# Decoder trunk layer in split fp32: the weight-half buffers made four deep and the block product regrouped

## The reference

```
h = rmsnorm(x)
parts = split(h @ w_in)                 # 46 tiles of 128 features for four mixers, and 64 of gate logits
o_a, o_b, o_c, o_d = hgrn2(...), diff_attention(...), nsa(...), chunk_gmlp(...)   # 512 wide each
merged = sum_b sigmoid(gate_b) * (o_b @ w_branch[b])
x = x + merged @ w_out
x = x + cross_attention(rmsnorm(x), rmsnorm(mem))     # 4 heads, 256 memory tokens
gate, up = split(rmsnorm(x) @ w_ffn_in) # 5632 each
x = x + (silu(gate) * up) @ w_ffn_out
out = rmsnorm(x)
```

## Time and profile before

| | |
|---|---|
| runs | 2203.86 us median of 3 (2201.33 to 2205.67) |
| profiled execution, span | 2204.4 us (its own time outside the span isn't recorded) |
| PE, PEld busy | 2090.2 us (95%), 1782.6 us (81%) |
| DVE, ACT, POOL busy | 1382.8 us (63%), 936.6 us (42%), 1063.7 us (48%) |
| memory traffic | 378.20 MB, mean 172 GB/s |
| granted TensorE clock | full, but for short stretches in the first 520 us and the end |

### The profile page before, as it was taken

One profiled execution on the slowest core, in us unless ns is written; L12 is line 12 of the kernel. 1 busy time (PEld: TensorE's weight loads), 2 busy tenths in 40 slices (PEclk: granted clock), 3 DMA queues, 4 the chain that ended last, 5 costly groups with the idle time before them and its releaser, 6 DMA issues.

```text
span 2204.4 us, 31459 instructions
## 1 busy us (share of the span) xinstructions
PE 2090.2 (95%) x11734; PEld 1782.6 (81%) x11734; DVE 1382.8 (63%) x1528; ACT 936.6 (42%) x1126; POOL 1063.7 (48%) x360
## 2 busy tenths in 40 slices
PE   6999988988999999999999999999999999999997
PEld 5788867877788888788888888888888888888886
DVE  7469876667555545585633337877777777744454
ACT  4354434443444444454433444444444444433332
POOL 3455455433444544445455442355555555555553
PEclk9999999989999999999999999999999999999999
DMA  5444544335455545554555444555555555565553
GB/s 206 147 158 160 174 153 164 129 115 175 153 173 178 180 168 176 210 172 172 179 184 173 152 153 150 212 173 183 179 173 185 174 177 185 171 229 177 186 190 115
DMA packets 53209, 378.20 MB, mean 172 GB/s; under 512 B 6160, under 2 KB 6416, under 8 KB 8464
## 3 DMA queue, kind: packets, MB, share of 16 engines
q1 hardware_dynamic: 50688, 365.71, 48.4%
q10 hardware_dynamic: 2448, 11.48, 1.3%
HBM read 372.98 MB, written 4.19 MB: 171 GB/s over the span
## 4 chain that ended last, share of the span: by engine, by line
PE 40%; issue 29%; POOL 18%; DVE 9%; ACT 3%; POOLq 0%; DMA 0%; DVEq 0%; ACTq 0%
PE acc L1382 23%; POOL w_lo L336 18%; PE acc L1383 12%; DVE w_lo L826 3%; ACT w_hi L408 2%; PE m L1461 1%; PE m L1790 1%; PE m L1766 1%; ACT probs L459 1%; DVE da_w L961 0%; DVE diag L856 0%; DVE x_weighted_split L1136 0%; PE m L1484 0%; PE m L1586 0%; DVE row_max L945 0%
## 5 line engine op out<-in xcount | busy, mean ns | idle before, releaser
L336 POOL TENSOR_TENSOR w_lo<-raw,w_hi 128x768 fp32r<-128x768 f32 (+3 forms) x346 | 1055.9, 3053 | 1107.6 <-ACT w_hi L408 1107.5
L1382 PE MATMUL acc<-x_split,w_hi 128*128 128x512 f32 x3344 | 1200.8, 402 | 35.5 <-DVE w_lo L826 19.4
L1383 PE MATMUL acc<-x_split,w_lo 128*128 128x256 f32 x3344 | 939.0, 281 | 0.0
L826 DVE TENSOR_TENSOR w_lo<-raw,w_hi 128x1280 fp32r<-128x1280 f32 (+3 forms) x346 | 575.6, 1664 | 373.6 <-ACT w_hi L408 370.1
L1382 PEld LDWEIGHTS acc<-x_split,w_hi 128*128 128x128 f32 x3344 | 631.9, 189 | 211.4 <-issue 56.3
L408 ACT ACTIVATE w_hi<-raw 128x2048 fp32r<-128x2048 f32 x346 | 660.8, 1911 | 109.0 <-PE acc L1383 102.0
L1383 PEld LDWEIGHTS acc<-x_split,w_lo 128*128 128x128 f32 x3344 | 634.9, 190 | 0.5 <-issue 0.3
L418 ACT ACTIVATE evac_half<-acc 128x256 f32<-128x256 f32 x358 | 136.0, 384 | 942.8 <-PE acc L1383 939.7
L1382 PE MATMUL acc<-mem_split,w_hi 128*128 128x512 f32 x768 | 275.0, 402 | 1.8 <-DVE mem_split L1264 0.7
L1382 PE MATMUL acc<-ffn_split,w_hi 128*128 128x512 f32 x704 | 249.9, 399 | 0.4 <-POOL w_lo L336 0.4
L1383 PE MATMUL acc<-mem_split,w_lo 128*128 128x256 f32 x768 | 215.0, 280 | 0.0
(11 more groups left out here) (294 smaller groups left out, 1509.2 us busy)
## 6 DMA issues: line engine op xcount, KB each, us to landing
raw<-in_w_fi SPq DMA_DIRECT2D x88, 1024.0 KB, 4.9
raw<-in_w_gate_b SPq DMA_DIRECT2D x60, 1024.0 KB, 4.9
raw<-in_w_start SPq DMA_DIRECT2D x54, 1024.0 KB, 5.0
raw<-in_w_fo SPq DMA_DIRECT2D x44, 1024.0 KB, 4.9
raw<-in_w_kv SPq DMA_DIRECT2D x32, 1024.0 KB, 4.9
raw<-in_w_gate_a SPq DMA_DIRECT2D x16, 1024.0 KB, 4.9
raw<-in_w_out SPq DMA_DIRECT2D x16, 1024.0 KB, 4.9
raw<-in_w_q SPq DMA_DIRECT2D x16, 1024.0 KB, 4.9
```

The source lines that it names most:

```text
L336: pool.tensor_tensor(w_lo(n)[:, b:TB], RAW[:, rs, b:TB], w_hi(n)[:, b:TB].bitcast(F32), ALU.subtract).then_inc(lo_pool, 1)
L826: dve.tensor_tensor(w_lo(n)[:, 0:b], RAW[:, rs, 0:b], w_hi(n)[:, 0:b].bitcast(F32), ALU.subtract).then_inc(lo_dve, 1)
L1382: pe.matmul(acc[bank][:], w_hi(n)[:, c], x, start=start, stop=False)
L1383: return pe.matmul(acc[bank][:, 0:S], w_lo(n)[:, c], x[:, 0:S], start=False, stop=stop)
```

## The change

The low half takes the raw's place: `w_lo` is laid over `raw` with four slots, `w_hi` gets four slots too, and the third pair of buffers, `evac_half` and `branch_now` go. Conversion runs two tiles ahead everywhere (AHEAD = 2) and `hi` waits for nothing but the raw tile. DVE makes 8 of 16 blocks in tiles 16 to 69 and 10 from 70 on. A block is three matmuls of 256 columns into one sum of 256 columns; the step that takes a result out of PSUM reads it once: ACT's copy, ACT's tanh (gates), DVE's multiply (merge, FFN), or DVE's residual add. Which engine takes which result out is a list (EVAC_BY), with one semaphore per engine. The FFN's token scale is copied from PSUM to SBUF (`ffn_scale`) once, and DVE waits for two spill transfers before it. The gb loop of TensorE is 3 rounds of 4 instead of 6 of 2, and the fo loop is written out.

```diff
+EVAC_BY = ["act"] * (len(PRODUCT_OF) + 16) + ["dve"] * 16 + (["act"] * 4 + ["dve"] * 4) * 12
+EVAC_BY += ["dve"] * 16 + ["act"] * 48 + ["dve"] * (16 + 2 * FC + DC)
+EVAC_NO = [EVAC_BY[:_i + 1].count(_by) for _i, _by in enumerate(EVAC_BY)]
...
-def slot_of(t):
-
-    return (t - 14) % 3 if WIDE0 <= t < WIDE1 else t % 2
...
+AHEAD = 2
...
-    if t is not None and WIDE1 <= t < WIDE1 + 5:
-        return 6
-    if t is None or not WIDE0 <= t < WIDE1:
-        return 10
-    if t < GA0 and START[t][0] == "cmp":
-        return 8
-    return 6 if 36 <= t < GA0 else 4
+    return 10 if t is None or not WIDE0 <= t < WIDE1 else 8
...
         RAW = sb("raw", 0, [P, RAWS, TB, P])
-        WHI = sb("w_hi", 32, [P, 2, TB, P], F32R)
-        WLO = sb("w_lo", 48, [P, 2, TB, P], F32R)
+        WLO = sb("w_lo", 0, [P, RAWS, TB, P], F32R)
+        WHI = sb("w_hi", 32, [P, RAWS, TB, P], F32R)
...
-        WHI3 = sb("w_hi3", 112, [P, TB, P], F32R)
-        WLO3 = sb("w_lo3", 120, [P, TB, P], F32R)
...
+        def wait_evac(engine, g):
+
+            by, no = EVAC_BY[g[2]], EVAC_NO[g[2]]
+            if known(g):
+                engine.wait_ge(evacuated[by], no)
+            else:
+                engine.wait_ge(evacuated[by], g[0] * EVAC_BY[g[2]:g[2] + g[1]].count(by) + no)
...
-                if not known(n):
-                    act.wait_ge(mm_done, val(n, -1))
-                elif last_user(n[2]) is not None:
-                    act.wait_ge(mm_done, last_user(n[2]) + 1)
                 act.activation(w_hi(n), RAW[:, rs], ACT.Copy).then_inc(hi_done, 1)

-            def half(tile, g):
+            def evac(tile, g, dst):

                 act.wait_ge(mm_done, val(tile, 1))
-                half_out(g)
...
+                act.activation(dst, acc[g[2] % ACCS][:, 0:S], ACT.Copy).then_inc(evacuated["act"], 1)
+
+            def gate(tile, g, dst):
+
+                act.wait_ge(mm_done, val(tile, 1))
+                act.activation(dst, acc[g[2] % ACCS][:, 0:S], ACT.Tanh, scale=0.5).then_inc(evacuated["act"], 1)
...
-            def residual(g, dst):
+            def residual(tile, g, dst):

-                dve.wait_ge(half_done, val(g, 1))
-                seq(dve.tensor_tensor(dst, dst, EV[:, g[2] % ACCS], ALU.add))
-                dve.tensor_tensor(dst, dst, acc[g[2] % ACCS][:, 0:S], ALU.add).then_inc(evac_done, 1)
+                dve.wait_ge(mm_done, val(tile, 1))
+                dve.tensor_tensor(dst, dst, acc[g[2] % ACCS][:, 0:S], ALU.add).then_inc(evacuated["dve"], 1)
...
                 for b in range(4):
-                    evac(plus(g, b), RB[:, b])
...
-                    dve.scalar_tensor_tensor(RB2[:, b] if b else dst, gates(b), 1.0, RB[:, b],
-                                             ALU.add, ALU.mult).then_inc(sem("merge"), 1)
+                    dve.scalar_tensor_tensor(RB2[:, b] if b else dst, gates(b), 1.0, acc[(g[2] + b) % ACCS][:, 0:S],
+                                             ALU.add, ALU.mult).then_inc(evacuated["dve"], 1)
...
             token_stats("n2", D, EPS, DGF)
+            dve.wait_ge(sem("spread"), spread("n2"))
+            seq(dve.tensor_copy(FSC[:], M[2][:, 0:S]))
+            for g in (1, 2):
+                dve.wait_ge(sem(f"x_spilled{g}"), 16)
...
-                evac(g, FG[:, par])
...
-                dve.tensor_tensor(FG[:, par], FG[:, par], M[2][:, 0:S], ALU.mult).then_inc(sem("ffn_gate"), 1)
-                lo(plus(t, 2))
+                dve.wait_ge(mm_done, val(t, 1))
+                dve.tensor_tensor(FG[:, par], acc[g[2] % ACCS][:, 0:S], FSC[:], ALU.mult).then_inc(evacuated["dve"], 1)
+                lo(plus(t, 1 + AHEAD))
...
-                pe.matmul(acc[bank][:], w_hi(n)[:, c], x, start=start, stop=False)
+                pe.matmul(acc[bank][:, 0:S], w_hi(n)[:, c], x[:, 0:S], start=start, stop=False)
+                pe.matmul(acc[bank][:, 0:S], w_hi(n)[:, c], x[:, S:2 * S], start=False, stop=False)
                 return pe.matmul(acc[bank][:, 0:S], w_lo(n)[:, c], x[:, 0:S], start=False, stop=stop)
...
-            with pe.Fori(0, 6) as i:
-                for j in range(2):
+            with pe.Fori(0, 3) as i:
+                for j in range(4):
...
-            with pe.Fori(0, 2) as i:
-                for blk in range(n // 2 * TB):
-                    tile, g = (i, n // 2, first + blk // TB), (i, DC // 2, g0 + blk // FC)
...
+            for blk in range(n * TB):
+                tile, g = at(first + blk // TB), at(g0 + blk // FC)
```

More of the change, by code:

```diff
@@ L355, in _ @@
             for t in range(WIDE1):
-                for u in ahead(t) if t else ():
-                    lo(at(u))
+                lo(at(t + AHEAD))
                 if t == 37:
@@ L378, in _ @@
             for t in range(4):
-                lo(at(first + t + 1))
+                lo(at(first + t + AHEAD))
                 if t == 0:
@@ L596, in start_step @@
             def start_step(t):
-                for u in ahead(t) if t else ():
-                    hi(at(u))
-                if t > GA0:
-                    gate_tanh(t - GA0 - 1)
+                hi(at(t + AHEAD))
                 if 1 <= t <= 4:
@@ L629, in _, with merged_hi @@
                 mixers(t)
-            def branch(tile, g, before):
-                for b in range(3):
-                    act.wait_ge(sem("branch_mm"), before + (b + 1))
-                    half_out(plus(g, b))
-                half(tile, plus(g, 3))
-            def merged_hi(ops, buf, j):
-                act.wait_ge(sem("merge"), ops)
+            def merged_hi(tiles, buf, j):
+                act.wait_ge(sem("merge"), tiles * 3)
                 act.activation(MGS[:, j, 0:S], MG[:, buf], ACT.Copy, scale=0.5).then_inc(sem("mg_hi"), 1)
@@ L650, in _ @@
                 else:
-                    merged_hi(7 * j, (j - 1) % 2, j - 1)
-                branch(at(first + j), at(g0 + 4 * j), 3 * j)
+                    merged_hi(j, (j - 1) % 2, j - 1)
             first, n, g0 = PHASES["gb"]
@@ L657, in _ @@
                         tile, g = (i, 20, first + 5 * j + b), (i, 32, g0 + 8 * j + b)
[L658 removed]
+                        hi(plus(tile, AHEAD))
                         if b == 0:
[L660 to L669 removed]
+                            merged_hi(i * 4 + (4 + j), (j + 3) % 2, i * 4 + (3 + j))
+                        gate(tile, g, GE[:, b])
+                    hi((i, 20, first + 5 * j + 4 + AHEAD))
             act.dma_start(MEM[:], a["mem"]).then_inc(sem("mem_in"), 16)
[L671 to L672 removed]
+            hi(at(PHASES["wo"][0] + AHEAD))
+            merged_hi(16, 1, 15)
             first, n, g0 = PHASES["wo"]
@@ L677, in _ @@
                 if k:
-                    hi(at(first + k + 1))
+                    hi(at(first + k + AHEAD))
                 if k == 3:
@@ L687, in _ @@
                         norm_hi(name, k - k0 - 5, tmp, dst)
-                half(at(first + k), at(g0 + k))
-            steps("kv", skip=12)
+                if k >= n:
+                    evac(at(first + k), at(g0 + k), KV[:, k - n])
+            steps("kv", KV, skip=12)
             def values(q4):
@@ L716, in _ @@
                 h, step = (k - 4) // 4, k % 4
-                hi(at(first + k + 1))
+                hi(at(first + k + AHEAD))
                 if k >= 4 and step == 1:
                     xa_softmax(h)
-                half(at(first + k), at(g0 + k))
+                evac(at(first + k), at(g0 + k), QF[:, k])
                 if k < 4:
@@ L727, in _ @@
                         xa_out(h)
-            hi(at(first + n + 1))
+            hi(at(first + n + AHEAD))
             xa_out(2)
@@ L1277, in _ @@
                     xa_out(h)
-            lo(at(first + n + 1))
+            lo(at(first + n + AHEAD))
             xa_out(2)
@@ L1358, in _ @@
                         dve.wait_ge(sem("x2_in"), 16)
-                    residual(at(g0 + nt), X2[:, nt])
+                    residual(at(first + t), at(g0 + nt), X2[:, nt])
             weigh(DC - 1)
```

223 lines of the change are left out of this document (85 added, 138 removed).

## The result

The changed kernel takes 2165.85 us (median of 4 runs, 2164.93 to 2236.38; the last of them, 2236.38, was a disturbed run and is left out of the ratio). Before: 2203.81 (2201.33 to 2205.67). The ratio is 0.982, 95% interval 0.981 to 0.984: 38 us faster, where the prediction had 101 and its range ended at 2160. The profiled execution has a span of 2164.0 us, 40.4 less than before.

The account below looks back on a forecast made before the run. The prediction saw a matmul stream stalling a little at tile borders on weight halves. Stalls of 56.5 + 5 + 0.8 + 13 = 75.3 us and 25 of blocks gave 2204.4 - 100.7 = 2103.7, say 2103; range 2058 to 2160.

Parts of the forecast that it names:

- gb: Gate and branch loop, 60 tiles: 22 of 25.6 us of border stalls would go.
- Part 4: Matmul block: three matmuls of 256 columns instead of 512 plus 256 take 0.346 us, not 0.351; saving 25 us.
- slower pattern: Earlier trace's slower matmul slots, 0.12 us for 256 columns; three gave 0.36 a block, taken as upper bound, +49 us.
- The first rival: Matmul blocks: splitting saves nothing or costs a little, 0.351 to 0.354 us, stalls still go; 2129 to 2145 us; chance 0.15.
- third rival: TensorE stream: load and matmul pairs can't be sustained; slower overall from a block of 0.365 us on; chance 0.05.
- The stalls: TensorE's stalls over all stages: 56.5 + 5 + 0.8 + 13 = 75.3 us would go.
- Opening and ga: Opening and first gates: 13 of 44 us of TensorE idle time would go, bounds 0 and 25.
- fi and fo: FFN in: 19 of 24.0 us of stalls go; FFN out: 3 of 7.4; 0.8 at the very end.
- wo and b1: Output projection with keys/values: 11 of 16.2 us of stalls go; first branch tiles: 5 of 10.
- Part 1: Weight halves four deep, low over raw, two tiles ahead: nearly all border stalls outside tiles 16 to 69 go, 56.5 us.
- Part 3: One PSUM read per result: 5 us in b1, 0.8 at the end, a share of the opening's 13, elsewhere nothing.

Follow-up runs that it names:

- the streams: A kernel of long matmul streams alone, no other engine at work: with 128-column weights, 512 columns took 0.227 us and 256 took 0.120.
- the reordering: Changed kernel with ScalarE's and VectorE's steps on the merged tile put ahead of the conversion, in b1 and before wo: 2159.79 us.
- the split alone: The kernel before with only the 512-column matmul cut in two of 256: 2230.55 us, 1.0125 of before.
- the two-deep one-step version: Changed kernel converting one tile ahead, with conversion of tile n waiting until tile n-2 ends, outside tiles 16 to 69: 2161.19 us.
- the changed kernel with 512 + 256: Changed kernel with blocks of one 512- and one 256-column matmul, only the first half of the bank read, one product left out: 2098.06 us.

## Why the prediction was wrong

**Part 4 failed**: "I take 0.346, nearer the pure 256 rows because they are the same stream width". The block measured 0.3599. The stream width was not all that mattered. Those rows had weights of 32 and 16 columns, and beside a load of 128 columns a 256-column matmul takes 0.120, alone or in the kernel. The row that had this very form was the earlier trace rows, 0.12 for today's 256-column matmul, and I had it as the upper bound and argued that it held only in a "slower pattern". The term was +50 us instead of -25: 75 us of error, more than the whole miss of 63. The first rival's price (block 0.351 to 0.354) was also too low; the case that came lies between it and my third rival, which begins at 0.365, and has the mechanism of neither: pairs as such can be sustained, at 0.112 with full loads of 128 or 240 columns. The fixed cost per matmul that the Trainium skill gives ("TensorE: Matmul & The Clock Gate", "Back-to-back issue gap") would be 13.5 us, an estimate; it has the sign, but the extra here isn't a constant per matmul: at 512 columns the streams took 0.227 us, at 256 either 0.113 or 0.120 by the size of the load.

**The stalls** were under-counted, 75.3 for 89.0. *Opening and ga*: 13 predicted, 38.3 measured, above my bound of 25. VectorE's new share accounts for 17 in these two stages (8.8 and 8.3 by the version with the old shares; 14 on the whole time), the one-step read for about 17 in the opening (108.6 against 91.2 over); the rest is open. The two don't simply add: with the old evacuation, depth and share together took 1.0 off the opening and 12.2 off ga. VectorE's L905 took 3.98 us in the earlier trace rows; it is L849 now and takes 2.89, as I had expected of it:

```profile
L849 DVE TENSOR_TENSOR hg_e<-hg_b 128x512 f32<-128x512 f32 x7 | 20.2, 2890 | 0.0
```

*fi and fo*: 22.8 predicted with the end, 27.3 measured. *gb*: 22 predicted, 15.2 measured, with 11 given back at two jumps that I hadn't seen coming; without them 26. *wo and b1*: 16 predicted, 6.2 measured with kv; the conversion two tiles on stands ahead of the merged step and holds it while a tile lands late (5.8 us at wo, by the reordering), where I had TensorE alone as late next.

**Part 1's sum was near, its reason half right.** The depth version, which has part 1 without parts 3 and 4 (and with VectorE's new share), took 60 us off the stages where I had 56.5. I put the border stalls down to the two slots. Shown: with the two-step read, four slots with one tile of lead have nearly the stalls of before (fi 22.5 us over, gb 23.1), so it is the lead that works, for which the third slot is needed; with the one-step read, two slots cost some 3 us (2161 against 2158, with overlapping ranges). "The path is ACT 1.91 us, then POOL 2.96 or more, with evacuation copies before it: over 5.2 of 5.62" was the right sum, but the copy was the part to look at. Part 3, which I costed at nothing outside the opening, takes away much of the same stalls by itself: from the split alone to the two-deep one-step version, fi goes from 18.0 to 2.3 us over, wo from 7.7 to 3.8, fo from 5.2 to 0.4 and gb from 19.7 to 12.5, 11 of which are the jumps; kv stays at 7.0. That holds for the tile of 5.76 us.

**Right**: waits on w_lo near zero behind the opening, no DMA or raw wait as a new limit (fi 1.6 us over), TensorE's instruction stream able to feed three pairs a block at this pace (written out, gb runs at exactly 5.76 a tile).

So of the 40.4 us: stalls -89 (about -100 without the jumps), third matmul +50. Depth and lead without the split give 2114, with the split where ScalarE and VectorE are short 2103; the change splits everywhere and pays 0.0092 to 0.0127 us a block for a read that, once conversion runs two tiles ahead, shows its main gain, some 17 us, in the opening, 46 of 338 tiles. That the stalls fell by more than I said made up for some 14 us of the 75: two errors against each other, which is luck.

Left open: why a load of 128 columns adds 6.7 ns at 256 columns; why the 512 + 256 block moves between 0.3465 and 0.3533 from stage to stage and version to version; and at what length of the body, between 1408 and 1920 loads and matmuls, the jump becomes slow, and by what.

## What to carry to other kernels

Price a matmul form by a row with the same stream width *and* the same size of weight load; if the trace has it only inside a mixed pattern, take that slot, not a cleaner stream of another shape. A producer that waits at every tile for its consumer, in front of the next conversion, closes a loop: add up the loop against the tile time before crediting buffers, since shortening the loop below the tile and giving a tile more lead are substitutes. Use the expensive form only in the stage where what it buys shows.

## What was unexpected of the hardware

- The gb loop of TensorE, whose body the change made from 10 tiles of two pairs a block (640 loads and matmuls) into 20 tiles of three (1920), stood for 3.1 us at each jump back, its branch instruction recorded at 4.95 and 4.88 us. The other versions that keep this loop have 4.8 to 5.1 us. Bodies of 640, of 960 (the split alone), of 1280 (the changed kernel with 512 + 256) and of 1408 (fo before) have 0.21 to 0.23 us. After the pause the clock was granted at 0.50 for some microseconds.
- Slots of 0.112 for 128 and 240 columns, 0.120 for 256 and 0.125 for 272, all with full loads: the two below 256 columns are alike, and 256 is already above the 0.1133 that smaller loads allow.
- The 512 + 256 block: 0.353 us in the mean by itself, with no other engine at work, and 0.3472 in the changed kernel with 512 + 256, although 0.2267 and 0.120, the two forms by themselves, make 0.347.
- The 128x512 add of VectorE: 3.98 us beside GpSimd pieces of 3.70 us and 2.89 beside pieces of 2.83, where the same form at L901 before and L845 after takes 0.69.
